# Modulation units of the attention stages taken as pairs of half contractions

## What is computed

```
m = silu(cond) @ w_mod + b_mod            # w_mod: 1024 x 6144, cond: two vectors (context, latent)
shift1, scale1, gate1, shift2, scale2, gate2 = split(m, 6)
h = rmsnorm(x) * (1 + scale1) + shift1    # then four mixers from h @ w_in: retention,
                                          # windowed, differential and latent attention
mixed = sum_n sigmoid(h @ w_gate[n] + b_gate[n]) * (mixer_n @ w_branch[n])
x = x + gate1 * (mixed @ w_out)           # then the gated MLP with shift2, scale2, gate2
```

## Time and profile before

| what | us |
|---|---|
| median of 3 runs (2322.63 to 2325.72) | 2324.95 |
| span of the profiled execution | 2320.6 |
| PE busy in it | 2286.9 (99%) |
| DVE busy | 1272.8 (55%) |
| ACT busy | 926.8 (40%) |
| POOL busy | 747.8 (32%) |

### The profile page before, as it was taken

One profiled execution on the slowest core, in us unless ns is written; L12 is line 12 of the kernel. 1 busy time (PEld: TensorE's weight loads), 2 busy tenths in 40 slices (PEclk: granted clock), 3 DMA queues, 4 the chain that ended last, 5 costly groups with the idle time before them and its releaser, 6 DMA issues.

```text
span 2320.6 us, 40593 instructions
## 1 busy us (share of the span) xinstructions
PE 2286.9 (99%) x17116; PEld 2061.5 (89%) x17116; DVE 1272.8 (55%) x2230; ACT 926.8 (40%) x1767; POOL 747.8 (32%) x498
## 2 busy tenths in 40 slices
PE   7999999999999999999999999999999999999998
PEld 6888898888989998998988879888889899899897
DVE  4446458644336763763663473685444467547556
ACT  3335346633335331331363352555442443223223
POOL 0331321111333544543422303121123435544442
PEclk9999999999999999999999999999999999999999
DMA  9313222223232324223242142222232332222211
GB/s 326 130 57 122 75 95 81 78 75 122 96 115 73 91 91 128 73 91 123 78 143 69 39 134 91 86 67 92 74 110 84 108 91 74 75 71 77 87 60 68
DMA packets 221907, 221.62 MB, mean 96 GB/s; under 512 B 10583, under 2 KB 191391, under 8 KB 221471
## 3 DMA queue, kind: packets, MB, share of 16 engines
q1 hardware_dynamic: 212999, 193.77, 26.2%
q10 hardware_dynamic: 8727, 25.27, 3.2%
HBM read 209.90 MB, written 9.11 MB: 94 GB/s over the span
## 4 chain that ended last, share of the span: by engine, by line
PE 92%; DVE 3%; ACT 3%; issue 1%; POOL 1%; DMA 0%; SPq 0%; POOLq 0%; DVEq 0%; ACTq 0%
PE ps L896 50%; PE ps L1027 12%; PE ps L1562 11%; PE ps L1484 4%; PE ps L1168 3%; PE ps L1185 2%; PE ps L916 1%; PE ps L1129 1%; PE ps L1144 1%; PE ps L992 1%; PE ps L1114 1%; PE ps L1150 1%; PE ps L1386 1%; PE ps L907 1%; POOL w_lo L855 1%
## 5 line engine op out<-in xcount | busy, mean ns | idle before, releaser
L855 POOL TENSOR_TENSOR w_lo<-raw,w_hi 128x512 fp32r<-128x512 f32 (+1 forms) x486 | 737.6, 1548 | 1550.7 <-ACT w_hi L1634 996.8
L896 PE MATMUL ps<-h_hi,w_hi 128*128 128x320 f32 (+2 forms) x2368 | 615.2, 312 | 0.0
L896 PE MATMUL ps<-h_lo,w_hi 128*128 128x320 f32 (+2 forms) x2368 | 607.0, 309 | 0.0
L896 PE MATMUL ps<-h_hi,w_lo 128*128 128x320 f32 (+2 forms) x2368 | 606.7, 309 | 0.0
L896 PEld LDWEIGHTS ps<-h_hi,w_hi 128*128 128x128 f32 x2368 | 412.8, 188 | 7.1 <-issue 4.6
L896 PEld LDWEIGHTS ps<-h_lo,w_hi 128*128 128x128 f32 x2368 | 413.4, 188 | 0.2
L896 PEld LDWEIGHTS ps<-h_hi,w_lo 128*128 128x128 f32 x2368 | 413.3, 188 | 0.0
L1634 ACT ACTIVATE w_hi<-raw 128x2048 fp32r<-128x2048 f32 (+2 forms) x110 | 203.8, 1852 | 268.5 <-PE ps L1562 94.6
L1562 PE MATMUL ps<-w_hi,a_hi 128*128 128x512 f32 x440 | 172.3, 392 | 0.6 <-POOL w_lo L855 0.6
L2646 DVE TENSOR_SCALAR conv<-u_pad,vcol 128x642 f32<-128x642 f32 x88 | 90.1, 1024 | 150.9 <-ACT u_pad L2071 149.3
L1562 PE MATMUL ps<-w_lo,a_hi 128*128 128x512 f32 x440 | 171.3, 389 | 0.0
(11 more groups left out here) (347 smaller groups left out, 3474.0 us busy)
## 6 DMA issues: line engine op xcount, KB each, us to landing
raw<-in_w_mod SPq DMA_DIRECT2D x44, 1024.0 KB, 5.1
raw<-in_w_up SPq DMA_DIRECT2D x88, 512.0 KB, 4.8
raw<-in_w_gate SPq DMA_DIRECT2D x32, 1024.0 KB, 5.3
raw<-in_w_in SPq DMA_DIRECT2D x16, 1024.0 KB, 5.2
raw<-in_w_down SPq DMA_DIRECT2D x16, 1024.0 KB, 5.1
w_br<-in_w_branch ACTq DMA_DIRECT2D x8, 1024.0 KB, 4.9
raw<-in_w_out SPq DMA_DIRECT2D x8, 1024.0 KB, 5.0
raw<-in_w_down SPq DMA_DIRECT2D x8, 768.0 KB, 4.4
```

Source lines behind the costliest of these rows:

```text
L855: ins = nc.gpsimd.tensor_tensor(w_lo[part_slot(li, s)][:, c0:c1], raw[HOME[u]][:, c0:c1], w_hi[part_slot(li, s)][:, c0:c1].bitcast(F32), A ...
L896: ins = mm(out, w_at(w_hl[wi]), at_(x_hl[xi]), start=first and q == 0, stop=final and q == 2)
```

## The change

From unit 8 on, a unit of modulation is four blocks of the contraction by 512 columns instead of eight by 256, and two units in a row, 2q and 2q + 1, hold the two halves of the contraction for the same 512 columns. They form a pair and are taken in one fill, `mod_halves`, at the step of the odd unit: 2 x 16 products of 32 rows by 128 columns (each two instructions on PE), with the sum going on in PSUM from the first half to the second. `mod_mm` is raised after each half. Then DVE transposes 128x128 from PSUM to PSUM and adds the bias (`take_halves`). The copies of rows on ACT and the folding products on PE are gone. The pairs stand at steps 6, 11 and 17 of the first attention, 6 and 14 of the second, 6, 14 and 20 of the third. The list of units, its order, the buffers, the other fills and the steps of rounding stay as they are.

```diff
 def fill_order(br):
...
-    mod, row = (lambda k: ("mod", at + k)), (lambda k: ("mod_row", at + k))
+    mod = lambda k: ("mod", (at + k) // 2)
     if br == 1:
-        return [[gate(10)], [branch(0), gate(11)], [branch(1)], [branch(2), mod(0)], [row(0), branch(3)], [gate(12)],
-                [branch(4), mod(1)], [branch(5), row(1)], [branch(6), mod(2)], [branch(7), row(2)], [branch(8), gate(13)], [branch(9), mod(3)],
...
+        return [[gate(10)], [branch(0), gate(11)], [branch(1)], [branch(2)], [branch(3)], [gate(12)],
+                [branch(4), mod(1)], [branch(5)], [branch(6)], [branch(7)], [branch(8), gate(13)], [branch(9), mod(3)],
...
-        items[where:where] = [mod(k), row(k) if at + k < DIRECT_MOD else None]
+        items[where:where] = [mod(k) if k % 2 else None, None]
...
+            if kind == "mod" and i >= 8:
+                return cut(a["w_mod"][one, i % 2 * 512:(i % 2 + 1) * 512, i // 2 * 512:(i // 2 + 1) * 512]), 4, 512
...
+                def mod_halves(q):
+
+                    c0 = mod_col(q)
+                    for half in range(2):
+                        w = raw_unit("mod", 2 * q + half)
+                        for k4 in range(4):
+                            k = 4 * half + k4
+                            turns = w[:, k4, :].rearrange("p (b g j) -> p g b j", g=4, j=32)
+                            for g in range(4):
+                                last = mm(ps[32 * g:32 * g + 32, c0:c0 + P].rearrange("p (b j) -> p b j", j=32),
+                                          cond_c[:, k, 2:34], turns[:, g], start=k == 0, stop=k == KD - 1)
+                        last.then_inc(mod_mm.sem, 1)
...
-                            if kind == "mod" and q < DIRECT_MOD:
-                                take_row(q)
...
+                def take_halves(q):
+
+                    ve.wait_ge(mod_mm.sem, now(mod_mm, 2 * q + 2))
+                    V.transpose(ps[:, mod_col(q) + P:mod_col(q) + 2 * P], ps[:, mod_col(q):mod_col(q) + P]).then_inc(vstep.sem, 1)
+                    ve.wait_ge(vstep.sem, step())
+                    tt(mod[:, 4 * q:4 * q + 4, :], ps[:, mod_col(q) + P:mod_col(q) + 2 * P].rearrange("p (b r) -> p b r", b=4)[:, :, 0:2],
+                       vcol[:, BMOD + 4 * q:BMOD + 4 * q + 4].unsqueeze(2).to_broadcast([P, 4, 2]), ALU.add).then_inc(mod_done.sem, 1)
```

More of the change, by code:

```diff
@@ L79 @@
 MLP = mlp_order()
-CONST_COLS = dict(ident=P, side=2, fold=4, colf=1, colb=1, mprev=P, mnext=P, dpos=P, upf=P, dneg=P, upb=P, rowf=P, rowb=P,
+CONST_COLS = dict(ident=P, side=2, colpad=4, colf=1, colb=1, mprev=P, mnext=P, dpos=P, upf=P, dneg=P, upb=P, rowf=P, rowb=P,
                   c16=NL * 64, s16=NL * 64, c8=NL * 32, s8=NL * 32)
@@ L253, in fill_order @@
     branch = lambda c: ("branch", 16 * n + c)
[L254 removed]
+    mod = lambda k: ("mod", (at + k) // 2)
     if br == 1:
[L256 to L258 removed]
+        return [[gate(10)], [branch(0), gate(11)], [branch(1)], [branch(2)], [branch(3)], [gate(12)],
+                [branch(4), mod(1)], [branch(5)], [branch(6)], [branch(7)], [branch(8), gate(13)], [branch(9), mod(3)],
+                [], [branch(10)], [branch(11)], [branch(12)], [], [branch(13), mod(5)], [],
                 [gate(14)], [gate(15)], [branch(14)], [branch(15)]]
@@ L673, in left_bank @@
             kind, q = item
-            if kind == "mod" and q >= DIRECT_MOD:
-                return mod_done, q - 3
-            return {"gate": (g_out, q + 1), "branch": (b_read, q + 1), "mod": (row_done, q - 7), "mod_row": (mod_done, q - 3)}[kind]
+            return {"gate": (g_out, q + 1), "branch": (b_read, q + 1), "mod": (mod_done, q + 1)}[kind]
         block = ctx.enter_context(nc.Block())
@@ L708, in unit_cols @@
             return k * n
-        unit_shape = [(kind,) + {"mod": (8, 256), "uq": (2, 384), "ukv": (1, 512), "gate": (8, 256),
+        unit_shape = [(kind,) + {"mod": (4, 512) if kind == "mod" and i >= 8 else (8, 256), "uq": (2, 384), "ukv": (1, 512), "gate": (8, 256),
                                  "out": (4, 512), "up": (8, 256), "in": (4, G_COLS[i[0]][1] if kind == "in" else 0),
@@ L897, in product3 @@
                     return ins
[L899 to L908, removed]
                 def mod_rows(layer, i, c0):
@@ L942, in mod_ahead @@
                     mod_rows(li + 1, MOD_ORDER[n], ahead_col(n))
[L944 to L951, removed]
                 def turn_channels(k):
@@ L1100, in fill @@
                         pe.wait_ge(sig.sem, now(sig, count))
-                    mod_form = mod_direct if item[0] == "mod" and item[1] >= DIRECT_MOD else mod_unit
-                    {"gate": gate_chunk, "branch": branch_chunk, "mod": mod_form, "mod_row": mod_transpose}[item[0]](item[1], **part)
+                    {"gate": gate_chunk, "branch": branch_chunk, "mod": mod_halves}[item[0]](item[1], **part)
                 def attention(br, ahead=None):
@@ L1308, in _ @@
                 pe.wait_ge(b_read.sem, now(b_read, 16))
-                pe.wait_ge(mod_done.sem, now(mod_done, 10))
+                pe.wait_ge(mod_done.sem, now(mod_done, 7))
                 in_product(4)
@@ L1350, in slot @@
                         pe.wait_ge(b_read.sem, now(b_read, 32))
-                        pe.wait_ge(mod_done.sem, now(mod_done, 14))
+                        pe.wait_ge(mod_done.sem, now(mod_done, 9))
                     if k >= 4:
@@ L1453, in _ @@
                 pe.wait_ge(b_read.sem, now(b_read, 48))
-                pe.wait_ge(mod_done.sem, now(mod_done, 20))
+                pe.wait_ge(mod_done.sem, now(mod_done, 12))
                 for v in range(2):
@@ L1649, in round_quarter @@
                         nxt[0] += 1
[L1651 to L1656, removed]
                 def row_rms(which, t, junk):
@@ L2386, in attention @@
                                 take_branch(q)
[L2387 to L2390, removed]
+                            if kind == "mod":
+                                take_halves(q)
                 if li:
@@ L2594, in _ @@
                 attention(3)
-                ve.wait_ge(mod_done.sem, now(mod_done, 20))
+                ve.wait_ge(mod_done.sem, now(mod_done, 12))
                 scale(1, 0, 8)
```

21 lines of the change are left out of this document (2 added, 19 removed).

## The result

The changed kernel takes 2360.26 us in the median (2357.87 to 2360.77), the one before 2323.88 in the same comparison: a ratio of 1.0157, 95% interval 1.0145 to 1.0169. It is slower, as forecast, by 36 us where 19 were forecast, and lies above the range. The span of the profiled execution is 2358.4 us, 37.8 more than before.

What follows compares the result with a forecast made beforehand. PE, busy 99% of the span, was taken as the bound. Per layer -3.7 + 4.75 + 2.2 + 4.5 + 1.7 = +9.45 us, both +18.9: span 2339.5, plus 4.35 for the median, said as 2344; range 2330 to 2352.

Steps and rivals of the forecast that it cites:

- The three long gaps: New PE idle gaps a layer, step 10 of first attention, 16 of the others: about 5.4, 2.2 and 4.5 us.
- The pair's price: PE time of one pair of modulation units: taken as 1.9 us, between 1.86 and 2.06.
- In(3,0): First attention's weight load, third of three, lands about T + 11.3 (T: pair's start); PE idles 5.4 us instead of 0.65.
- gate(2,0): Second attention's weight load, waiting for a pair's first half, takes 5.2 us; PE idles 2.2 us where it had none.
- gate(3,0): Third attention's weight load, behind unit 22 on SP, takes 7.2 us as second of two; PE idles 4.5 us.
- part 3, the clock: Half-clock stretches behind the new gaps in the attentions: one a layer, between none and three, losing 1.7 us.
- The rival of more clock: Each of the three gaps brings its half-clock stretch, 5.1 us a layer, the run 2350.6 us; chance 0.17.
- part 2 on DVE: DVE's transposition from PSUM to PSUM hides beside PE: nothing, between a gain and a loss of 0.3 us a pair.
- part 1: Work taken from PE by pairing units and dropping foldings: saves 3.7 us a layer, 7.4 in both.
- the sum: All terms together: +9.45 us a layer, +18.9 in both, taking the profiled span from 2320.6 to 2339.5 us.

Runs made afterwards that it cites:

- e1: Changed kernel with three roundings put later (in(3,0) at step 12 instead of 8, gate(2,0) and gate(3,0) at 16 instead of 14): 2335.47 us, ratio 1.0046.
- e2: Changed kernel with each pair at the step of its even unit instead of the odd one: 2334.46 us, ratio 1.0045.
- e3: Kernel before, with both single units one behind the other at the odd unit's step, all in the form without row copies and foldings: 2363.07 us, ratio 1.0165.
- e8: The kernel of e1 with DVE taking the pairs of the first attention one step later: 2326.64 us, ratio 1.0008.
- e10: Kernel before without foldings in the first attention, its units whole at their own steps, with DVE taking them one step later: 2320.20 us, ratio 0.9979.
- e5: The kernel of e1 with PE products nobody reads added ahead of five scores of the first attention: 2334.01 us, ratio 1.0039.

## Why the prediction was wrong

**The direction and the places were right.** The three long gaps stand where they were put, behind the three roundings, and come from late buffers: e1, e2 and e3 each show it, from different sides. The pair's price was right as well: 1.88 us for 1.9.

**The long gaps' sizes** were 4.00, 2.86 and 5.89 us for 5.4, 2.2 and 4.5, in sum 12.75 for 12.1. In(3,0) landed as forecast, but 1.37 us of its gap moved ahead, to the scores before, where PE stood by DVE's wait. For gate(2,0) I took a load alone, 5.2 us; it took 6.0, since the loads of uq and gate(2,1) went out right behind it. For gate(3,0) I counted two loads together, 7.2 us; the second half of the pair released unit 23 as a third, and it took 8.6.

**The step that failed first is part 3, the clock.** The term was 1.7 us a layer and measured 7.1 in the first and 6.5 in the second. The mechanism was right, the count and the length were not: all three gaps brought a stretch, two of them twice as long as the price I took, the one of 6.5 us in the second layer three times. The rival of more clock had the count, but at 5.1 us a layer not the length. My argument against it (PE goes from a gap into dense work) fell: behind the gaps of 4.07 and 2.71 us in the second layer PE worked 3.4 us of 3.4, at half clock. The run that kept PE at work in the gaps shows that 6.7 us of the run, 8.5 by the spans, hang on it. The rule of the Trainium skill named in the prediction ("TensorE: Matmul & The Clock Gate", Part 1), an array left idle falls to 1.2 GHz, agrees with the two longest gaps, for which I had it bring a stretch; the third, of 2.86 us, brought one as well.

**The second is part 2 on DVE: "I give it nothing between a gain and a loss of 0.3 us a pair".** I looked at how long the transposition takes (0.33 us, near enough) and not at what DVE waits for ahead of it and what is queued behind that. It waits 1.69 us, the next head's maximum stands behind, and the exponent behind that. In the first attention this is 2.5 us with late rounding, and without foldings 4.5 us in the first layer and 3.4 in the second, as e8 and e10 show.

**The third is part 1: a microsecond taken from PE's row of work as a microsecond of the run.** 99% busy was read as bound everywhere. Where the way from scores to exponent has become longer, as in the first attention, PE's work only fills it, and e5 shows 6.8 us of added work to be free in the gaps. Of the 3.9 us saved in a layer nothing arrived: with the stalls taken out (e1), the attentions of the first layer were 307.6 us long, 5.2 more than the 302.4 before. But PE's work isn't free in this attention whatever the kernel: in e10, where DVE's wait is taken away, it has 1.7 us less of it than in the kernel before (67.51 for 69.21) and is 2.0 us shorter (68.8 for 70.8). The second and third together are the small gaps: 4.2 us a layer beside the long ones, and 8.8 once these are gone (e1: 12.2 for 3.4). DVE's wait is shown for 2.5 of these 8.8; that missing fills make the rest is argued, not shown.

The page tells how the misses add up. The span grew by 37.8 us where the sum had 18.9. PE stood idle 34.7 us more (68.4 for 33.7) where the sum had 2 x 11.45 = 22.9, and was busy 3.1 us more where it had 2 x (3.7 - 1.7) = 4.0 less: 11.8 and 7.1 us, 18.9 in all. The idle part is mostly small gaps, 2 x 4.85 (4.2, and the 0.65 us that the sum had taken off the gap of in(3,0)), and 1.8 for the long gaps, which came to 12.75 and 13.3 us for 12.1. In the busy part the stretches in the attentions lost 10.2 us more than the sum had; against that stand 1.4 us for a stretch less in the start, 1.7 for the one of 1586.78, which the changed kernel doesn't have, and 0.4 for the cheaper pair. The median missed by less, 16.3 us, and that is luck: it lies 1.9 us above the profiled span here, and the sum had added the 4.35 us of before.

## What to carry to other kernels

When a step is moved on an engine that works in order, ask of every engine that takes part what it now waits for and what is queued behind that wait: a buffer that comes free later holds up the loads behind it, and a result fetched at the end of its own step, instead of the next, holds up the work of the next head. An engine that is 99% busy need not be what sets the pace in each stage once the change is in; put work that nobody reads into its gaps, and if the time stays, it isn't PE's work that sets the pace there. And price an idle gap of PE with the clock behind it: the three gaps of 2.9 to 5.9 us in the first layer cost half as much again.

## What the runs showed of the hardware

The six gaps of PE of 2.7 to 6.5 us in the changed kernel's attentions were each followed by a stretch of 3.4 to 10.2 us at a granted clock of 0.50, and products without a use in these gaps made the kernel 7 us faster. Shorter gaps were followed by one at times: the same gap of 1.81 us (pairs at the even step) in the first layer and not in the second, one of 2.3 us (late rounding) in the second and not in the first. And two stretches of the kernel before stood behind 3.4 us of PE's work without a gap. Three 1 MB loads that went out within 1 us landed 5.0, 7.1 and 9.1 us after their issues. DVE transposed 128x128 from PSUM to PSUM in 0.33 us.
